# A scan kernel's first product of C and B, moved from behind the transposes into the middle of the next tile's product

## The chip, the cores and the metric

The kernel runs on one core of a Trainium2 chip. The metric is the device time of one execution in microseconds (us). Three executions of the kernel before took 4853.73 to 4854.49 us, with a median of 4853.85 us.

## What is computed

The reference is one layer of a hybrid block: a normalized input goes through one large projection, whose columns feed a state-space scan (SSD) and a second scan (HGRN2); both are mixed, and a large table of experts is applied after that. The change concerns only the SSD scan. Cut to it:

```python
z, xbc, dt_raw, hq, hf, hi, hg, gate_s, gate_h = jnp.split(h @ w_in, split_at, axis=-1)
xbc = jax.nn.silu(causal_dwconv(xbc, conv_w, conv_b))
xs, bm, cm = jnp.split(xbc, [SSD_D_INNER, SSD_D_INNER + SSD_N_GROUPS * SSD_D_STATE], axis=-1)
...
# ssd_chunked, for each of 8 groups of 4 heads, in 4 chunks of 128 tokens
cb = jnp.einsum('bclgn,bcsgn->bgcls', cc, bc)
y_diag = jnp.einsum('bgrcls,bcsgrp->bclgrp', cb[:, :, None] * lmat, xc)
states = jnp.einsum('bcsgn,bgrcs,bcsgrp->bcgrpn', bc, decay_states, xc)
...
y_off = jnp.einsum('bclgn,bcgrpn,bgrcl->bclgrp', cc, states, jnp.exp(a_cum))
```

`cb` is the product of C and B of one chunk (128x128 for one group). It is weighted with the decays of the group's four heads and multiplied with x.

## The kernel before

The SSD stage works through 8 groups in 10 rounds `u`. In round `u`, TensorE makes the six projected tiles of group `u` (`s` = 0 to 5; a tile is 128 features by 512 tokens, 16 steps of 3 matmuls, 48 in all), while the scan of group `p = u - 1` (`comp`) and the end of group `f = u - 2` (`fin`) run between them. Round 0 and round 1 are written out; rounds 2 to 7 are a hardware loop with one body; round 8 has no projection any more, but has six tiles of a gate in its place. So a scan runs in rounds 1 to 8: the first, six in the loop, the last.

**Weights.** A tile of weights comes by a DMA that SP issues into `ring_raw` (two slots). ACT copies it, rounded, to `ring_high` (`split_high`, L258), POOL (GpSimd) subtracts that from the raw tile and writes `ring_low` (`split_low`, L263). TensorE may start a tile once its low half is there (`ring.low_ready`). In ACT's program `split_high` of tile `s + 1` stands at the head of step `s`; in step 1 of a round with `fin` it is followed by the tanh of tile 1 and by `rooted_squares`, a logarithm and an exponential of group `f`. For tile 3 ACT's `split_high` comes right behind those.

**The scan of a group on TensorE.** Behind tile 0 and tile 1 TensorE transposes two tiles of x, behind tile 2 it transposes B (`turn`, L660, into `ps_turn`). VectorE (DVE) copies B out to `b_tok` (L907, counted by `turned_read`). `part_a(p, c)` (L666) is the product of C and B for chunk `c`, and goes into the same `ps_turn`, so it waits for that copy. `part_b(p, c)` (L678 to L684) multiplies the weighted scores with x, and the state; it waits for `mixed_ready`. After tile `s` from 3 on, `part_b(p, s - 3)` and `part_a(p, s - 2)` follow.

**VectorE.** In step 2 it does, in this order: the copy to `b_tok`, the convolution of tile 2 (L808, L810), a sigmoid (L819), `mix(p, 0)` and `make_spans(p, 1)` (L836). Then come step 3's sigmoid and the convolution of tile 3. `mix` waits for ACT's decays and for `part_a`, and is this:

```python
chain.after(v.tensor_tensor(scores[:], ps_turn[:, 0:CH], const["upto"], ALU.mult))
v.tensor_tensor(mixed[:], decay[:], scores[:].unsqueeze(1).to_broadcast([P, HPG, CH]), ALU.mult)
if c < NC - 1:
    v.tensor_tensor(x_dec[:], xdt[:, c].rearrange("p (h d) -> p h d", h=HPG),
                    decay[:, :, CH - 1:CH].to_broadcast([P, HPG, HD]), ALU.mult)
    v.tensor_copy(chunk_dec[:], decay0[:, :, CH - 1])
v.tensor_tensor(c_dec[:], decay0[:],
                act_in[:, 3, c * CH:(c + 1) * CH].unsqueeze(1).to_broadcast([P, HPG, CH]),
                ALU.mult).then_inc(mixed_ready, 1)
```

**ACT.** In steps 2 and later it makes tanh of tile `s`, then the two decays of chunk `s - 2` (L598, L600), and then, at the head of the next step, `split_high` of tile `s + 2`. None of these waits for `part_a(p, 0)`; the decays of chunk 1 wait for `mixed_ready` of chunk 0.

Of the kernel before, what the change touches and what calls it, by code (L numbers as in the profile page):

```python
# [273 lines left out]
def product(nc, out, high, low, x_high, x_low, steps=range(KT), tokens=slice(0, T),  # L274
            wait_piece=None):

    for k in steps:
        if wait_piece is not None and k % PIECE == 0:
            wait_piece(k // PIECE + 1)
        m = slice(k * P, (k + 1) * P)  # L280
        nc.tensor.matmul(out, high[:, m], x_high[:, k, tokens], start=(k == 0), stop=False, skip_group_check=True)  # L281
        nc.tensor.matmul(out, high[:, m], x_low[:, k, tokens], start=False, stop=False, skip_group_check=True)  # L282
        last = nc.tensor.matmul(out, low[:, m], x_high[:, k, tokens], start=False, stop=(k == KT - 1),  # L283
                                skip_group_check=True)
    return last
# [87 lines left out]
def ssd_stage(nc, dram, ring, sent, h, const, streams, norm_mix_w, in_rstd, sums_dram, y_out, gates_out, following):  # L373
# [7 lines left out]
    with ExitStack() as ctx:  # L381
# [54 lines left out]
        turned_read = sem("turned_read")  # L436
# [175 lines left out]
        def _(pe):  # L612
# [7 lines left out]
            def first_tile():  # L620

                pe.wait_ge(ring.low_ready, ring.base + 1)
                pe.wait_ge(acc_read, 1)
                for k in range(KT):
                    pe.wait_ge(x_low, k + 1)
                    tile_done = product(nc, acc[0][:], ring.high[:, 0], ring.low[:, 0], h[0], h[1], range(k, k + 1))
                    if k == DT_FROM:
                        pe.wait_ge(dt_low, 1)
                    for j in range((k - DT_FROM) * KT // (KT - DT_FROM), (k - DT_FROM + 1) * KT // (KT - DT_FROM)):
                        if j >= 0:  # L630
                            dt_done = dt_step(j)
                tile_done.then_inc(ring.used, 1)
                dt_done.then_inc(dt_summed, 1)

            def turn_dt():
                pe.wait_ge(dt_kept, 1)
                for c in range(NC):
                    last = nc.tensor.transpose(ps_turn[:, c * SSD_HEADS:(c + 1) * SSD_HEADS],
                                               y_sq[0:SSD_HEADS, 0, c * CH:(c + 1) * CH],
                                               const["ident"][0:SSD_HEADS, 0:SSD_HEADS])  # L640
                last.then_inc(dt_turned, 1)

            def sum_steps():
                pe.wait_ge(adt_ready, 1)
                for c in range(NC):
                    last = nc.tensor.matmul(ps_turn[0:SSD_HEADS, c * CH:(c + 1) * CH], adt[:, c], const["upto"],
                                            start=True, stop=True)
                last.then_inc(adt_summed, 1)

            def turn_sums():  # L650
                pe.wait_ge(sums_kept, 1)
                for c in range(NC):
                    last = nc.tensor.transpose(ps_turn[:, c * SSD_HEADS:(c + 1) * SSD_HEADS],
                                               sum_rows[:, c * CH:(c + 1) * CH],
                                               const["ident"][0:SSD_HEADS, 0:SSD_HEADS])
                last.then_inc(sums_turned, 1)

            def turn(dst, src, done):
                for c in range(NC):
                    last = nc.tensor.transpose(dst[:, c * P:(c + 1) * P], src[:, c * CH:(c + 1) * CH],  # L660
                                               const["ident"])
                last.then_inc(done, 1)

            def part_a(p, c):
                tok = slice(c * CH, (c + 1) * CH)
                nc.tensor.matmul(ps_turn[:, 0:CH], act_in[:, 2, tok], act_in[:, 3, tok],  # L666
                                 start=True, stop=True).then_inc(a_done, 1)

            def part_b(p, c):
                pe.wait_ge(mixed_ready, NC * p + c + 1)  # L670
                if c == 0:
                    pe.wait_ge(y_read, p + 1)
                else:
                    pe.wait_ge(state_ready, (NC - 1) * p + c)
                for head in range(HPG):
                    part = slice(HD * (head % 2), HD * (head % 2) + HD)
                    o = ps_y[head // 2][part, c * CH:(c + 1) * CH]
                    last = nc.tensor.matmul(o, xdt[:, c, head * HD:(head + 1) * HD], mixed[:, head],  # L678
                                            start=True, stop=(c == 0), skip_group_check=True)
                    if c > 0:  # L680
                        last = nc.tensor.matmul(o, state[:, head], c_dec[:, head], start=False, stop=True,
                                                skip_group_check=True)
                if c < NC - 1:
                    last = nc.tensor.matmul(ps_state[:], b_tok[:, c], x_dec[:].rearrange("p h d -> p (h d)"),  # L684
                                            start=True, stop=True)
                last.then_inc(b_done, 1)

            def body(u, proj, comp, fin, first=False):
                p, f = u - 1, u - 2
                for s in range(SSD_TILES):  # L690
                    n = SSD_TILES * u + s
                    if first and s == 0:
                        first_tile()
                        continue

                    def half(i):
                        return product(nc, acc[s % 2][:], ring.high[:, s % 2], ring.low[:, s % 2], h[0], h[1],
                                       range(i * KT // 2, (i + 1) * KT // 2))

                    def sum_squares():  # L700
                        pe.wait_ge(squared, f + 1)
                        pe.wait_ge(rooted, f + 1)
                        for t in range(2):
                            last = nc.tensor.matmul(ps_squares[:], const["ones"], y_sq[:, t],
                                                    start=(t == 0), stop=(t == 1))
                        last.then_inc(summed, 1)

                    if proj or early(u, s):
                        pe.wait_ge(ring.low_ready, ring.base + n + 1)
                        i = 0 if proj else SSD_TILES * (u - G) + s  # L710
                        if i < 2:
                            pe.wait_ge(acc_read, n + 1)
                        else:
                            pe.wait_ge(gate_read, i - 1)
                        half(0)
                    if s == 0 and fin:
                        part_b(f, NC - 1)
                    if s == 1 and fin and not comp:
                        sum_squares()
                    if first and s == 1:  # L720
                        turn_dt()
                    if first and s == 3:
                        sum_steps()
                    if first and s == 5:
                        turn_sums()
                    if proj or early(u, s):
                        half(1).then_inc(ring.used, 1)
                    if s == 0:
                        if comp:
                            pe.wait_ge(in_ready, p + 1)  # L730
                            turn(ps_turn, act_in[:, 0], turned)
                    if s == 1:
                        if fin and comp:
                            sum_squares()
                        if comp:
                            pe.wait_ge(turned_read, 3 * p + 1)
                            turn(ps_turn, act_in[:, 1], turned)
                    if comp:
                        if s == 2:
                            pe.wait_ge(turned_read, 3 * p + 2)  # L740
                            turn(ps_turn, act_in[:, 2], turned)
                            pe.wait_ge(turned_read, 3 * p + 3)
                            part_a(p, 0)
                        if s > 2:
                            part_b(p, s - 3)
                            part_a(p, s - 2)

            body(0, True, False, False, True)
            body(1, True, True, False)
            with pe.Fori(2, G) as u:  # L750
# [1944 lines left out]
```

## Time and profile before

| | |
|---|---|
| median of 3 runs | 4853.85 us |
| the profiled execution | 4859.09 us |
| its span, first to last instruction | 4857.3 us |
| TensorE (PE) busy | 4780.7 us, 98% of the span |
| VectorE (DVE) busy | 3168.6 us, 65% |
| ACT busy | 1579.4 us, 33% |
| POOL busy | 1316.1 us, 27% |
| mean granted TensorE clock | 0.994 |
| first and last product of C and B (L666) | 146.0 and 720.5 us from the span's start |

The rows give times from the start of the span. "PEld" is TensorE's weight load, which can run beside the matmul ahead of it. A bracket at the end of a row tells how long the engine had been idle before it, and what released it.

### The profile page before, as it was taken

To read this page: it belongs to the slowest core of one execution; us is meant where nothing else is said; L and a number is where in the kernel's file an instruction comes from. 1 tells how busy PE (TensorE), PEld (TensorE's weight loads), DVE (VectorE), ACT (ScalarE), POOL (GpSimd) and SP (SyncE) were. 2 spreads that over 40 slices of the span, in tenths; PEclk is the share of its full clock that TensorE was granted. 3 is DMA by queue.
4 is the path that set the end of the run, shared out by engine and by line. 5 is a ranking of instruction groups with operands and counts; after the bars stand their busy time and mean duration, and the time that the engine had idled before them with its cause. 6 is when DMAs were issued, how large, how long until landed. Compare 5 with 4: busy or idle time off the path is not lost. (4 is left out here: it accounts for less than half of the span.)

```text
span 4857.3 us, 64058 instructions
## 1 busy us (share of the span) xinstructions
PE 4780.7 (98%) x23758; PEld 4133.8 (85%) x23758; DVE 3168.6 (65%) x4246; ACT 1579.4 (33%) x1534; POOL 1316.1 (27%) x549
## 2 busy tenths in 40 slices
PE   8999999999999999999999999999999899999998
PEld 6777788888888787888879999999999788888887
DVE  5676666888878501001168866667674698888888
ACT  3223333333333312212232268822222222222221
POOL 2333330000000043444434442266662111111110
PEclk9999999999999999999999999999999999999999
DMA  3233233222222334334233378799996898888885
GB/s 124 91 108 109 93 122 109 91 82 98 86 94 95 119 125 167 110 127 175 95 129 114 113 246 279 279 339 336 340 340 221 319 337 318 306 297 308 310 297 201
DMA packets 269597, 928.81 MB, mean 191 GB/s; under 512 B 38576, under 2 KB 129200, under 8 KB 191952
## 3 DMA queue, kind: packets, MB, share of 16 engines
q1 hardware_dynamic: 214224, 659.32, 38.9%
q0 software_dynamic: 55296, 268.53, 15.6%
q8 instruction: 41, 0.67, 0.1%
q14 instruction: 36, 0.29, 0.0%
HBM read 849.25 MB, written 78.51 MB: 191 GB/s over the span
## 5 line engine op out<-in xcount | busy, mean ns | idle before, releaser
L263 POOL TENSOR_TENSOR ring_low<-ring_raw,ring_high 128x2048 fp32r<-128x2048 f32 x161 | 754.3, 4685 | 2080.5 <-ACT ring_high L258 2080.5
L281 PE MATMUL rt_acc<-h_high,ring_high 128*128 128x384 f32 (+1 forms) x2304 | 790.8, 343 | 5.9 <-POOL ring_low L263 3.2
L282 PE MATMUL rt_acc<-h_low,ring_high 128*128 128x384 f32 (+1 forms) x2304 | 785.1, 341 | 0.0
L283 PE MATMUL rt_acc<-h_high,ring_low 128*128 128x384 f32 (+1 forms) x2304 | 784.9, 341 | 0.0
L258 ACT ACTIVATE ring_high<-ring_raw 128x2048 fp32r<-128x2048 f32 x337 | 644.9, 1914 | 392.1 <-PE mix_s_acc L283 126.8
L281 PEld LDWEIGHTS rt_acc<-h_high,ring_high 128*128 128x128 f32 x2304 | 433.3, 188 | 18.8 <-DVE h_low L301 5.0
L283 PEld LDWEIGHTS rt_acc<-h_high,ring_low 128*128 128x128 f32 x2304 | 433.2, 188 | 10.4
L282 PEld LDWEIGHTS rt_acc<-h_low,ring_high 128*128 128x128 f32 x2304 | 433.4, 188 | 9.4
L281 PE MATMUL hg_acc<-h_high,ring_high 128*128 128x512 f32 x1088 | 433.6, 399 | 2.1 <-DVEq L1253 1.6
L283 PE MATMUL hg_acc<-h_high,ring_low 128*128 128x512 f32 x1088 | 425.6, 391 | 0.0
L282 PE MATMUL hg_acc<-h_low,ring_high 128*128 128x512 f32 x1088 | 423.9, 390 | 0.0
L2238 DVE TENSOR_TENSOR ring_low<-ring_raw,ring_high 128x2048 fp32r<-128x2048 f32 x107 | 245.3, 2293 | 263.4 <-ACT ring_high L258 263.4
L1743 POOL DMA_INDIRECT sb_op_rows<-v_tiles,row_of x128 | 120.7, 943 | 977.1 <-DVE x_tok_back L2429 849.8
L281 PE MATMUL ssd_acc<-h_high,ring_high 128*128 128x512 f32 x896 | 357.0, 398 | 9.1 <-DVE h_low L301 5.7
L282 PE MATMUL ssd_acc<-h_low,ring_high 128*128 128x512 f32 x896 | 350.5, 391 | 0.0
L283 PE MATMUL ssd_acc<-h_high,ring_low 128*128 128x512 f32 x896 | 350.5, 391 | 0.0
L2429 DVE SCALAR_TENSOR_TENSOR x_tok_back<-sb_op_rows,own_weight,x_tok_back 128x2048 f32<-128x2048 f32 x128 | 300.4, 2347 | 0.0
L1743 POOL DMA_INDIRECT x_mid_front<-u_rows,row_of x128 | 199.3, 1557 | 353.0 <-DVE sb_rt_dot L2219 332.5
L2219 DVE CUSTOM_DVE_ANT_0 x_mid_front<-x_mid_front,sb_rt_h_tok 128x2048 f32<-128x2048 f32 x128 | 292.7, 2287 | 0.0
L2453 DVE TENSOR_TENSOR x_tok_back<-x_tok_back,op_out 128x512 f32<-128x512 f32 x384 | 261.5, 683 | 43.4 <-PE op_out L2411 40.7
L1947 POOL DMA_INDIRECT gates_added<-sb_rt_added_gate,sb_rt_added_at x128 | 241.5, 1887 | 52.8 <-issue 37.8
L1976 ACT ACTIVATE sent_gelu<-rt_acc 128x384 f32<-128x384 f32 x128 | 63.0, 493 | 560.4 <-PE rt_acc L283 560.3
(330 smaller groups left out, 9683.8 us busy)
## 6 DMA issues: line engine op xcount, KB each, us to landing
ring_raw<-u_tiles SPq DMA_DIRECT2D x128, 1024.0 KB, 5.1
ring_raw<-v_tiles SPq DMA_DIRECT2D x128, 1024.0 KB, 6.2
ring_raw<-w_hg SPq DMA_DIRECT2D x64, 1024.0 KB, 4.9
ring_raw<-w_ssd SPq DMA_DIRECT2D x48, 1024.0 KB, 6.6
ring_raw<-w_mix_s SPq DMA_DIRECT2D x32, 1024.0 KB, 5.4
ring_raw<-w_mix_h SPq DMA_DIRECT2D x32, 1024.0 KB, 4.9
gelu<-sent_gelu SPq DMA_DIRECT2D x128, 192.0 KB, 4.9
weights_gelu<-gelu SPq DMA_DIRECT2D x32, 768.0 KB, 8.2
```

The source lines that it names most:

```text
L258: nc.scalar.activation(ring.high[:, slot], ring.raw[:, slot], ACT.Copy).then_inc(ring.high_ready, 1)
L263: nc.gpsimd.tensor_tensor(ring.low[:, slot], ring.raw[:, slot], ring.high[:, slot].bitcast(F32), ALU.subtract).then_inc(ring.low_ready, 1)
L281: nc.tensor.matmul(out, high[:, m], x_high[:, k, tokens], start=(k == 0), stop=False, skip_group_check=True)
L282: nc.tensor.matmul(out, high[:, m], x_low[:, k, tokens], start=False, stop=False, skip_group_check=True)
L283: last = nc.tensor.matmul(out, low[:, m], x_high[:, k, tokens], start=False, stop=(k == KT - 1), skip_group_check=True)
L1743: return pool.indirect_dma_start(rows[0:OWN, slot], None, table, bass.IndirectOffsetOnAxis(ap=row_of[0:OWN, k:k + 1], axis=0))
L1947: pool.indirect_dma_start(scratch["gates_added"].rearrange("i j (t a) -> (i j t) a", a=1), bass.IndirectOffsetOnAxis(ap=added_at[:, e:e + ...
L1976: nc.scalar.activation(gelu[:, s], acc[s][:, 0:REST], ACT.Gelu).then_inc(acc_read, 1)
L2219: vec.tensor_tensor_reduce(rows[0:OWN, slot], rows[0:OWN, slot], h_tok[0:OWN], 1.0, 0.0, ALU.mult, ALU.add, dot[0:OWN, slot:slot + 1]).the ...
L2238: vec.tensor_tensor(ring.low[:, slot], ring.raw[:, slot], ring.high[:, slot].bitcast(F32), ALU.subtract).then_inc(ring.low_ready, 1)
L2429: vec.scalar_tensor_tensor(x_tok[0:OWN, 0], rows[0:OWN, slot], weight[0:OWN, ds(k, 1)], x_tok[0:OWN, 0], ALU.mult, ALU.add).then_inc(summe ...
L2453: vec.tensor_tensor(x, x, ps_out[(2 * OUTS * buf + OUTS * half + i) % BANKS][:], ALU.add).then_inc(out_added, 1)
```

## The change

TensorE's product of C and B for the first chunk of a group, `part_a(p, 0)`, with its wait for the copy of B, is taken from behind the transposes of B at the end of step 2 and put between the two halves (24 matmuls each) of tile 3's product. Nothing is added or removed, and no other engine's program is changed; no DMA is moved.

```diff
@@ -715,6 +715,9 @@
                         half(0)
                     if s == 0 and fin:
                         part_b(f, NC - 1)
+                    if s == 3 and comp:
+                        pe.wait_ge(turned_read, 3 * p + 3)
+                        part_a(p, 0)
                     if s == 1 and fin and not comp:
                         sum_squares()
                     if first and s == 1:
@@ -739,8 +742,6 @@
                         if s == 2:
                             pe.wait_ge(turned_read, 3 * p + 2)
                             turn(ps_turn, act_in[:, 2], turned)
-                            pe.wait_ge(turned_read, 3 * p + 3)
-                            part_a(p, 0)
                         if s > 2:
                             part_b(p, s - 3)
                             part_a(p, s - 2)
```

TensorE's instructions in the loop's body, at the end of tile 2 and the start of tile 3, before the change (a REGISTER_ALU row works out the value that the next wait compares with):

```order
L283 MATMUL ssd_acc<-h_high,ring_low 128x512
L740 REGISTER_ALU
L660 MATMUL ssd_ps_turn<-c_ident,streams 128x128 x4
L742 REGISTER_ALU
L666 MATMUL ssd_ps_turn<-streams 128x128
L709 REGISTER_ALU
L281 MATMUL ssd_acc<-h_high,ring_high 128x512
```

The same place in the changed kernel:

```order
L283 MATMUL ssd_acc<-h_high,ring_low 128x512
L743 REGISTER_ALU
L660 MATMUL ssd_ps_turn<-c_ident,streams 128x128 x4
L709 REGISTER_ALU
L281 MATMUL ssd_acc<-h_high,ring_high 128x512
L282 MATMUL ssd_acc<-h_low,ring_high 128x512
```

The product L666 is gone from between the transposes and tile 3; the next wait of TensorE behind the transposes is now that of tile 3 itself. The middle of tile 3 in the changed kernel, with the 24th matmul of the tile in the second row:

```order
L282 MATMUL ssd_acc<-h_low,ring_high 128x512
L283 MATMUL ssd_acc<-h_high,ring_low 128x512
L719 REGISTER_ALU
L666 MATMUL ssd_ps_turn<-streams 128x128
L281 MATMUL ssd_acc<-h_high,ring_high 128x512
L282 MATMUL ssd_acc<-h_low,ring_high 128x512
```

There the product has arrived, 24 matmuls later in TensorE's order than before. At the end of tile 3 the order is as it was.

## Rows read from the trace of the kernel before

**Rows 1.** Waits of the weight loader, 120 to 740 us: us in total, times, longest

```profile
PEld ssd_ps_turn L666 <- DVE sb_ssd_b_tok L907: 8.2, 8, 1.0
...
PEld ssd_acc L281 <- POOL ring_low L263: 1.4, 6, 0.2
```

**Rows 2.** Timeline of PE, a loop round, from the transposes of B to tile 3

```profile
451.05 0.60 PE L660 MATMUL ssd_ps_turn<-c_ident,streams 128*128 128x128 f32 x4
452.43 0.49 PE L666 MATMUL ssd_ps_turn<-streams 128*128 128x128 f32 x2 [0.78 <-DVE sb_ssd_b_tok L907]
452.97 0.50 PE L281 MATMUL ssd_acc<-h_high,ring_high 128*128 128x512 f32 x1
453.31 0.40 PE L282 MATMUL ssd_acc<-h_low,ring_high 128*128 128x512 f32 x1
```

**Rows 3.** Timeline of PE, transposes of x behind tile 0, the same round

```profile
426.62 0.60 PE L660 MATMUL ssd_ps_turn<-c_ident,streams 128*128 128x128 f32 x4
...
427.29 0.40 PE L282 MATMUL ssd_acc<-h_low,ring_high 128*128 128x512 f32 x1
```

**Rows 4.** Timeline of POOL, the same round: low halves of tiles 3 and 4

```profile
448.35 4.57 POOL L263 TENSOR_TENSOR ring_low<-ring_raw,ring_high 128x2048 fp32r<-128x2048 f32 x1 [9.48 <-ACT ring_high L258]
459.36 4.65 POOL L263 TENSOR_TENSOR ring_low<-ring_raw,ring_high 128x2048 fp32r<-128x2048 f32 x1 [6.45 <-ACT ring_high L258]
```

**Rows 5.** Timeline of DVE, the same round: mix of chunk 0 and the spans

```profile
457.51 0.29 DVE L855 TENSOR_TENSOR sb_ssd_scores<-ssd_ps_turn,c_upto 128x128 f32<-128x128 f32 x1 [1.41 <-ACT sb_ssd_decay L600]
457.84 0.69 DVE L856 TENSOR_TENSOR sb_ssd_mixed<-sb_ssd_decay,sb_ssd_scores 128x512 f32<-128x512 f32 x1
...
458.85 0.69 DVE L861 TENSOR_TENSOR sb_ssd_c_dec<-sb_ssd_decay,streams 128x512 f32<-128x512 f32 x1
459.45 5.23 DVE L836 TENSOR_SCALAR sb_ssd_span_log<-sb_ssd_sums,sb_ssd_sum_at 128x128 f32<-128x128 f32 x4
```

**Rows 6.** Timeline of PE, the same round: middle of tile 3, then its end

```profile
458.58 0.39 PE L281 MATMUL ssd_acc<-h_high,ring_high 128*128 128x512 f32 x1
...
464.11 0.66 PE L678 MATMUL ssd_ps_y<-sb_ssd_mixed,sb_ssd_xdt 128*64 128x128 f32 x8
...
465.24 0.38 PE L666 MATMUL ssd_ps_turn<-streams 128*128 128x128 f32 x2
465.38 0.48 PE L281 MATMUL ssd_acc<-h_high,ring_high 128*128 128x512 f32 x1
465.69 0.39 PE L282 MATMUL ssd_acc<-h_low,ring_high 128*128 128x512 f32 x1
```

**Rows 7.** Timelines of DVE and POOL in round 1, from 113 us

```profile
115.31 5.52 DVE L883 TENSOR_TENSOR streams<-streams 128x1024 f32<-128x1024 f32 x1
...
113.70 6.04 POOL L263 TENSOR_TENSOR ring_low<-ring_raw,ring_high 128x2048 fp32r<-128x2048 f32 x1 [6.93 <-ACT ring_high L258]
```

**Rows 8.** Timelines of PE, DVE and POOL in round 1, first scan

```profile
144.63 0.60 PE L660 MATMUL ssd_ps_turn<-c_ident,streams 128*128 128x128 f32 x4
...
146.58 0.39 PE L282 MATMUL ssd_acc<-h_low,ring_high 128*128 128x512 f32 x1
...
150.77 0.29 DVE L855 TENSOR_TENSOR sb_ssd_scores<-ssd_ps_turn,c_upto 128x128 f32<-128x128 f32 x1 [1.40 <-ACT sb_ssd_decay L600]
...
152.62 4.63 POOL L263 TENSOR_TENSOR ring_low<-ring_raw,ring_high 128x2048 fp32r<-128x2048 f32 x1 [8.82 <-ACT ring_high L258]
```

**Rows 9.** Timelines of PE, DVE and POOL in round 8, last scan

```profile
682.67 0.47 PE L281 MATMUL ssd_acc<-h_high,ring_high 128*128 128x512 f32 x1
682.99 0.39 PE L282 MATMUL ssd_acc<-h_low,ring_high 128*128 128x512 f32 x1
...
683.02 0.29 DVE L855 TENSOR_TENSOR sb_ssd_scores<-ssd_ps_turn,c_upto 128x128 f32<-128x128 f32 x1 [0.65 <-PE ssd_ps_turn L666]
...
684.76 4.75 POOL L263 TENSOR_TENSOR ring_low<-ring_raw,ring_high 128x2048 fp32r<-128x2048 f32 x1 [5.54 <-ACT ring_high L258]
```

**Rows 10.** Window with all eight scans: busy us of each engine, PEclk, DMA

```profile
118.00:736.00 618.00, 611.45 (x3020) 491.89 (x3020) 403.12 (x557) 189.44 (x199) 228.96 (x50) 1.00 0.31 105
```

## The prediction

> **What bounds the kernel now.** I read the window over all eight scans first: TensorE is busy 611.45 of 618 us at a granted clock of 1.00 [rows 10], so a microsecond that TensorE is held there is a microsecond of the time. Then the waits of its weight loader [rows 1]: the product that the change moves stands idle eight times, 1.0 us each, for the copy of B. That is what the change goes after. The reader should see the row below it too: six times tile 3's first weights wait 0.2 us for POOL's low half. Small as it is, it says that in the six loop rounds tile 3 could not have started earlier, whatever stood in front of it. The timelines show it. POOL's subtraction for tile 3 runs from 448.35 to 452.92, and tile 3 starts at 452.97 [rows 4, 2]. In the first and the last scan there is no such wait.
>
> **What the change gives, by round.** Where nothing holds TensorE, it is 0.67 us from the start of four transposes to the second matmul of the next tile [rows 3]; behind the transposes of B it is 2.26 us [rows 2]. So 1.59 us stand there for the moved product and its wait.
> In the first scan this distance is 146.58 - 144.63 = 1.95 [rows 8]: without the product it should be 0.67, a gain of 1.28. The last scan's rows have the same form [rows 9]; I take 1.28 there too.
> In the six loop rounds I take a gain of nothing. TensorE comes to tile 3 at about 451.5 and waits for POOL until 452.97, as before. POOL's time is set by ACT, whose rounding copy for tile 3 stands behind the logarithm and the exponential of `rooted_squares`; all of that hangs on the end of tile 1, which the change does not touch.
>
> **What the product costs in its new place.** From L666 to the second matmul behind it is 465.69 - 465.24 = 0.45, when nothing is waited for [rows 6]. With one step of 0.23 from the matmul in front, that is 0.68 where two plain steps take 0.46, so 0.23 us. The bounds are 0.2 (its own streaming) and 0.65 (0.88 from L666 to the second matmul after a stop, in [rows 2]). I take 0.23: the copy of B is long done there, so no stop is due. First and last scan together: 2 x (1.28 - 0.23) = 2.1 us gained.
>
> **Who is late next.** `mix(p, 0)` on DVE waits for the product and for ACT's decays. Before, the product is early and the decays decide, at 457.51 [rows 5]. Now the product comes behind the 24th matmul, where a matmul starts at 458.58 [rows 6]. In the last scan the scores start 0.35 after the matmul that follows the product [rows 9], and that matmul follows it by 0.14 [rows 6]. So in a loop round the scores start at 458.58 + 0.14 + 0.35 = 459.07, which is 1.56 later.
> By itself this is harmless: `c_dec` would end at 459.54 + 1.56 = 461.1, and `part_b` asks for it only at 464.11 [rows 6], or 464.34 with the 0.23 above. But POOL starts its subtraction for tile 4 at 459.36 and ends at 464.01 [rows 4]; that time doesn't move, as nothing that ACT does before it waits for the product. Before, `mix` was just through: `c_dec` started at 458.85, and the spans behind it were caught, four small instructions in 5.23 us [rows 5]. Now `mixed`, the second instruction of `mix`, comes to 459.07 + 0.33 = 459.40, and finds POOL at work.
> Does a TENSOR_TENSOR wait for POOL as the spans do? One row says yes: L883, both inputs in SBUF, started at 115.31 with POOL's subtraction running from 113.70 to 119.74, and took 5.52 us [rows 7]. At `c_dec`'s pace (0.69 for 512 elements) its 1024 need 1.3, so it ran only from about POOL's end on. `mixed`, `x_dec` and `c_dec` have both inputs in SBUF as well.
> The Trainium skill, page "SBUF — State Buffer", section "Who interferes with whom", says that a DVE instruction with two SBUF inputs contends with a GpSimd instruction that reads SBUF, and that whichever is first keeps the other out to its end. By that rule `mixed` waits here, and the change loses in the loop; the trace agrees, with the 5.52 us of L883.
>
> So in a loop round `mixed` runs from about 463.9. From its start to the end of `c_dec` it is 459.54 - 457.84 = 1.70 [rows 5], so `mixed_ready` comes at 465.6, and `part_b` starts 1.5 us later than at 464.11. The 0.23 lie inside this. It doesn't matter much who wins at 459.36 against 459.40: if `mixed` slips in first, POOL starts up to 0.65 later, ends near 464.65, and `x_dec` to `c_dec` (1.09) end at 465.7.
> The bounds of this term: 0.23 (nobody blocks), 0.6 (only the COPY and the spans are blocked: `chunk_dec` waits, and `c_dec` ends at 464.7), and 2.3 (below).
> What is late behind it has cover: the convolution of tile 3 and with it ACT's decays, its split for tile 5 and POOL come some 1.9 us later, TensorE 1.5; and the next tile 3 is tied to its own tile 1.
>
> **First scan.** Tile 3's second matmul moves to 145.30, its 25th to 145.30 + (458.58 - 453.31) = 150.57, the scores to 151.06 instead of 150.77 [rows 8]. `c_dec` starts 1.34 after the scores, at 152.40, and POOL at 152.62: it just gets through. It then holds POOL up to 0.5, so tile 4's low half comes at about 157.7, and TensorE is there at 157.6. I take 0.1 off: 0.9 gained. If the 0.2 us of room are not there, `c_dec` ends near 157.9, where `part_b` stood at 146.58 + 10.80 = 157.4, and the scan loses 0.5 instead.
> **Last scan.** The scores come at about 687.5, inside POOL's subtraction (684.76 to 689.51 [rows 9]), so `mix` ends at 689.4 + 1.7 = 691.1. `part_b` asks at 681.7 + 10.8 + 0.2 = 692.7. No wait: 1.0 gained.
>
> **The sum.** 6 x 1.5 - 0.9 - 1.0 = 7.1 us more. The profiled execution took 4859.09, so 4866.2 by it; it stands 5.24 above the median of the runs, so 4861.0 for the median, 0.15% above 4853.85. No other stage is touched; they follow TensorE and shift with it.
>
> **The rivals.**
> - *Plain gain*, 0.04: TensorE's 1.0 us comes free in all eight, because POOL's row against tile 3 is a coincidence. 8 x 1.05 = 8.4 less: 4845.5. Against it: [rows 1] name POOL six times, exactly the loop rounds.
> - *Tile 3 is tied to POOL, but nobody blocks `mix`*, 0.04: 6 x 0.23 - 2.1 = -0.7: 4853.1. The 5.52 of L883 speaks against it.
> - *Only the COPY is blocked*, 0.08: 6 x 0.6 - 1.9 = 1.7: 4855.6. L883 speaks against it, but it is one row.
> - *A longer block*, slower, 0.09. Place: POOL's subtraction for tile 4. With a DVE instruction in front, POOL's took 6.04 us in [rows 7] instead of 4.65. If `mixed` slips in first and POOL takes that, it ends at 465.4, and `x_dec` to `c_dec` at 466.4: 2.3 a round, 6 x 2.3 - 1.9 = 11.9: 4865.8. It decides from 1.93 a round on, (9.7 + 1.9) / 6.
> - *The clock falls*, slower, 0.05: TensorE now stands twice in 13 us, about 1.5 before tile 3 and 1.3 behind it. If the granted clock fell to half for half a tile (5.5 us) each round, that would be 33 us: 4894. Before, eight waits of 1.0 us leave it at 1.00 [rows 10].
> - *My forecast*, 0.70, with a range of its own of 4858.5 to 4863.5 (1.1 to 1.9 a round; the first scan gains or loses).
>
> **How the numbers follow.** A measurement of this kernel can tell about 0.2%, 9.7 us, from no change. The range 4855 to 4866 takes in my forecast, the COPY rival and the longer block: 0.87, less some 0.05 at its edges. Faster by over 0.2% needs the plain gain and 1.2 us or more in each scan: 0.02. Slower by over 0.2% is the longer block, the clock, and a little of my own case: 0.16. Within 0.2%: 0.82.
>
> **What the changed profile would show.** In the loop rounds: tile 3's first matmul still directly behind POOL's end, now with about 1.4 us of waiting for POOL; the scores released by L666 and no longer by ACT; `mixed` (L856) with about 5.2 us instead of 0.69 in six rounds and in the last; `part_b` waiting about 1.3 us for `c_dec`; the period of a round 1.5 longer. In the first scan no long `mixed`. The prediction is wrong if `mixed` keeps 0.69 in the loop, if tile 3 starts earlier than POOL's end allows (then POOL was ahead), or if tile 5 or the next round picks up a new wait.

## The result, and the profile after

In 20 executions of each, the changed kernel takes a median of 4861.53 us (4857.83 to 4869.19) and the kernel before 4856.09 us (4851.88 to 4858.94). The medians are 5.4 us apart. The ratio is 1.0013 with a 95% interval of 1.0007 to 1.0019: slower by 0.13%, which is less than the 0.2% by which I called a change measurable, but the interval leaves out no change at all. The forecast was 4861.0 and 0.15%. That 4861.0 is so near to 4861.53 is in part luck: the forecast stood on 4853.85 for the kernel before, and its 20 executions came out 2.2 us above that. The difference was forecast as 7.1 us and measured as 5.4.

Single executions of one kernel spread by 7 to 11 us, so a profiled span can't be read for this change: that of after (4856.5 us) is even shorter than that of before. The stage itself repeats far better. I take as **the stage** the time from the first scan's first transposes (L660) to the last product of C and B (L666), both read on TensorE's timeline. Before it is 720.54 - 121.91 = 598.63 us, after it is 725.65 - 120.35 = 605.30 us: 6.67 more, where the forecast's sum was 7.1. Each stage is read from one trace, but its rounds repeat: from the transposes of B in one loop round to those in the next it is 76.62 to 76.70 us before.

The waits of TensorE and its weight loader in the changed kernel, 120 to 745 us (us in total, times, longest), with the shorter waits left out; they answer to [rows 1]:

```profile
PEld ssd_acc L281 <- POOL ring_low L263: 9.3, 6, 1.6
PEld ssd_ps_y L678 <- DVE sb_ssd_c_dec L862: 9.2, 6, 1.5
PE ssd_acc L281 <- POOL ring_low L263: 7.9, 6, 1.3
PE ssd_ps_y L678 <- DVE sb_ssd_c_dec L862: 6.7, 6, 1.1
```

The eight waits for the copy of B are gone. In six rounds POOL has taken their place in front of tile 3, and behind tile 3 six new waits for VectorE's `c_dec` have appeared. Below is one loop round on TensorE; the rows answer to [rows 2] and [rows 6], and lines of the changed file from 718 on have a higher number than before:

```profile
452.81 0.60 PE L660 MATMUL ssd_ps_turn<-c_ident,streams 128*128 128x128 f32 x4
454.73 0.50 PE L281 MATMUL ssd_acc<-h_high,ring_high 128*128 128x512 f32 x1 [1.32 <-POOL ring_low L263]
...
460.35 0.38 PE L666 MATMUL ssd_ps_turn<-streams 128*128 128x128 f32 x2
467.34 0.66 PE L678 MATMUL ssd_ps_y<-sb_ssd_mixed,sb_ssd_xdt 128*64 128x128 f32 x8 [1.12 <-DVE sb_ssd_c_dec L862]
```

The same round on VectorE, and POOL's subtraction for tile 4; they answer to [rows 5] and [rows 4]:

```profile
460.83 0.29 DVE L856 TENSOR_TENSOR sb_ssd_scores<-ssd_ps_turn,c_upto 128x128 f32<-128x128 f32 x1 [2.97 <-PE ssd_ps_turn L666]
461.16 5.12 DVE L857 TENSOR_TENSOR sb_ssd_mixed<-sb_ssd_decay,sb_ssd_scores 128x512 f32<-128x512 f32 x1
466.20 0.41 DVE L859 TENSOR_TENSOR sb_ssd_x_dec<-sb_ssd_xdt,sb_ssd_decay 128x256 f32<-128x256 f32 x1
466.54 0.16 DVE L861 COPY sb_ssd_chunk_dec<-sb_ssd_decay 128x4 f32<-128x4 f32 x1
466.61 0.68 DVE L862 TENSOR_TENSOR sb_ssd_c_dec<-sb_ssd_decay,streams 128x512 f32<-128x512 f32 x1
...
461.12 4.60 POOL L263 TENSOR_TENSOR ring_low<-ring_raw,ring_high 128x2048 fp32r<-128x2048 f32 x1 [6.45 <-ACT ring_high L258]
```

The scores are now released by the product and no longer by ACT, 8.02 us behind the start of the transposes of B (before 6.46). `mixed` meets POOL's subtraction 0.04 us after its start, and takes 5.12 us instead of 0.69.

That is the picture in two of the six loop rounds. In the other four `mixed` is the first of the two, by at most 0.03 us, and `x_dec` is caught in its place:

```profile
304.90 0.69 DVE L857 TENSOR_TENSOR sb_ssd_mixed<-sb_ssd_decay,sb_ssd_scores 128x512 f32<-128x512 f32 x1
305.51 4.83 DVE L859 TENSOR_TENSOR sb_ssd_x_dec<-sb_ssd_xdt,sb_ssd_decay 128x256 f32<-128x256 f32 x1
...
304.93 5.13 POOL L263 TENSOR_TENSOR ring_low<-ring_raw,ring_high 128x2048 fp32r<-128x2048 f32 x1 [6.46 <-ACT ring_high L258]
...
311.08 0.66 PE L678 MATMUL ssd_ps_y<-sb_ssd_mixed,sb_ssd_xdt 128*64 128x128 f32 x8 [1.11 <-DVE sb_ssd_c_dec L862]
```

POOL's instruction is then recorded with 5.13 us instead of 4.60, so it has waited for `mixed` in turn, and TensorE's wait is the same to 0.01.

### The profile page after: what moved, and what is told of

Its sections match the earlier page's. It is cut to its first block and busy times, and to the rows that moved or that the text cites. A ratio compares the mean times of both kernels' runs of the same rounds, so it can differ in the third digit from the quotient of the medians.

```text
span 4856.5 us, 64058 instructions
## 1 busy us (share of the span) xinstructions
PE 4771.5 (98%) x23758; PEld 4127.4 (85%) x23758; DVE 3169.8 (65%) x4246; ACT 1579.5 (33%) x1534; POOL 1315.8 (27%) x549
```

## The experiments

Each experiment is one more edit to one of the two kernels, timed beside the kernel before on the same chip. The table has the stage of each as its one trace shows it; what was expected stands with each below. Four kernels have intervals that take in 1: for them the times alone tell nothing, and the reading rests on the stage. In all eleven the difference of the stage and that of the medians agree within 1.3 us.

| kernel | stage, us | to before | ratio of times, 95% interval |
|---|---|---|---|
| before | 598.63 | | |
| the change | 605.30 | +6.67 | 1.0013 (1.0007 to 1.0019) |
| before, early rounding copy | 596.58 | -2.05 | 0.9996 (0.9987 to 1.0005) |
| change, early rounding copy | 588.86 | -9.77 | 0.9981 (0.9972 to 0.9990) |
| change in the outer two rounds alone | 596.52 | -2.11 | 0.9996 (0.9987 to 1.0005) |
| change in the six loop rounds alone | 607.36 | +8.73 | 1.0018 (1.0009 to 1.0027) |
| product behind the 12th matmul | 598.27 | -0.36 | 0.9999 (0.9990 to 1.0008) |
| product behind the 36th matmul | 609.48 | +10.85 | 1.0020 (1.0011 to 1.0029) |
| change, scores in PSUM | 601.92 | +3.29 | 1.0008 (0.9999 to 1.0017) |
| 12th matmul, early rounding copy | 588.66 | -9.97 | 0.9979 (0.9970 to 0.9988) |
| change, POOL held back | 614.97 | +16.34 | 1.0037 (1.0023 to 1.0050) |
| 36th matmul, early rounding copy | 616.99 | +18.36 | 1.0035 (1.0021 to 1.0049) |

### Which rounds gain and which lose

Two kernels have the product moved in some rounds only. `type(u) is int` holds for the written-out rounds, and the second kernel has the opposite:

```diff
-                    if s == 3 and comp:
+                    if s == 3 and comp and type(u) is int:
                         pe.wait_ge(turned_read, 3 * p + 3)
                         part_a(p, 0)
...
                             turn(ps_turn, act_in[:, 2], turned)
+                            if not (type(u) is int):
+                                pe.wait_ge(turned_read, 3 * p + 3)
+                                part_a(p, 0)
```

> The product is moved only in the two written-out rounds (first and last scan); the six loop rounds keep it behind the transposes. My theory: -1.0 in each of the two, nothing else: stage 596.6, time -2 us. Rival (the gain of the outer rounds is not there, the whole +6.67 of the stage is a smaller loss in all eight): 600.3.

> The product is moved only in the six loop rounds. My theory: +1.43 in each of six: stage 607.2, time +8.6 us (+0.18%). Rival (a smaller loss in all eight): 603.6.

Measured: 596.52 and 607.36. The loop rounds lose 1.45 each, and the two effects add up to the change: -2.11 + 8.73 = 6.62, against 6.67. A loss spread over all eight is out. What each outer round gains is read best from its own stretch. From the transposes of B in the first scan to those in the next round it is 76.35 us before and 75.36 with the product moved, so 0.99. From the last transposes of B to the last product of C and B it is 39.49 and 38.52, so 0.97. The other 0.15 of the 2.11 lies in the six rounds that this edit leaves alone; so small a difference in a stage means nothing.

### Is tile 3 held by POOL?

ACT's rounding copy of tile 3 is put ahead of tile 1's tanh and of the logarithm and exponential, in the loop rounds; first in the kernel before:

```diff
-                    if (proj or early(u, s)) and not (first and s == 0):
+                    ahead = proj and fin
+                    if (proj or early(u, s)) and not (first and s == 0) and not (ahead and s == 2):
                         split_high(nc, act, ring, (s + 1) % 2, SSD_TILES * u + s + 1, 3 * u + (s + 1) // 2)
+                    if ahead and s == 1:
+                        split_high(nc, act, ring, 1, SSD_TILES * u + 3, 3 * u + 1)
```

> The kernel before, with one change on ACT alone: in the six loop rounds the rounding copy of tile 3 (split_high) stands ahead of tile 1's tanh and of the logarithm and exponential, not behind them. I measure the stage in the trace from the first scan's first transposes (L660) to the last product of C and B (L666): 598.63 us before, 605.30 with the change. My theory (tile 3 is held by POOL's low half): tile 3 starts directly behind the product of C and B as in the first scan, 0.31 us earlier in each of six rounds: stage 596.7, time -1.9 us (-0.04%, not to be told in the times). Rival (tile 3 was not held by POOL): 598.6.

Measured: 596.58. The six waits for POOL are gone from the trace, and the stage is shorter by 2.05, 0.34 a round. So the 0.2 us of [rows 1] were a real hold on TensorE, and not a coincidence. How firm a bound POOL is shows when the product goes as well. The same edit in the changed kernel:

> The changed kernel with ACT's early rounding copy of tile 3 in the loop rounds. My theory: POOL is done some 8 us earlier, tile 3 starts behind the transposes, 1.59 us earlier than before, the product costs 0.23, the scores come at about the time at which ACT's decays are done, and mix is through before POOL's next subtraction: -1.36 in each of six rounds and -2.1 in the outer two: stage 588.4, time about -10 us (-0.2%). Room for c_dec ahead of POOL is some 0.5 us. Rival A (the block of mix has nothing to do with where tile 3 starts, it comes with the product's new place): mixed still takes 5.1 us in the loop and part_b waits: stage 598 to 600. Rival B (the early copy makes a new wait, on VectorE's sigmoid behind POOL's earlier subtraction, that reaches TensorE): over 590 with a wait of the transposes.

Measured: 588.86. TensorE waits in the stage neither for POOL nor for `c_dec`. VectorE and POOL in a loop round of this kernel:

```profile
451.10 0.29 DVE L859 TENSOR_TENSOR sb_ssd_scores<-ssd_ps_turn,c_upto 128x128 f32<-128x128 f32 x1 [1.41 <-ACT sb_ssd_decay L603]
451.43 0.69 DVE L860 TENSOR_TENSOR sb_ssd_mixed<-sb_ssd_decay,sb_ssd_scores 128x512 f32<-128x512 f32 x1
...
452.44 0.69 DVE L865 TENSOR_TENSOR sb_ssd_c_dec<-sb_ssd_decay,streams 128x512 f32<-128x512 f32 x1
...
452.95 4.62 POOL L263 TENSOR_TENSOR ring_low<-ring_raw,ring_high 128x2048 fp32r<-128x2048 f32 x1 [14.58 <-ACT ring_high L258]
```

The scores wait for ACT's decays again, `mixed` takes 0.69, and `c_dec` starts 0.5 us before POOL. The stage is 9.77 below that of the kernel before. Of these 2.05 are the early copy's own, and 7.72 are the moved product's: with tile 3 free to start, the same move that cost 6.67 gains 7.72. It is 0.96 in each loop round (76.34 to 75.38 us) and 0.98 and 0.97 in the outer ones. Rivals A and B are both out.

### Does the loss depend on where in tile 3 the product stands?

The product stands behind 12 or 36 of the tile's 48 matmuls instead of 24. The kernel for 12 (the changed kernel's product between the halves is taken out; the other likewise in the second half):

```diff
                     def half(i):
-                        return product(nc, acc[s % 2][:], ring.high[:, s % 2], ring.low[:, s % 2], h[0], h[1],
-                                       range(i * KT // 2, (i + 1) * KT // 2))
+                        steps = range(i * KT // 2, (i + 1) * KT // 2)
+                        if s == 3 and comp and i == 0:
+                            product(nc, acc[s % 2][:], ring.high[:, s % 2], ring.low[:, s % 2], h[0], h[1], range(0, 4))
+                            pe.wait_ge(turned_read, 3 * p + 3)
+                            part_a(p, 0)
+                            steps = range(4, KT // 2)
+                        return product(nc, acc[s % 2][:], ring.high[:, s % 2], ring.low[:, s % 2], h[0], h[1], steps)
...
-                    if s == 3 and comp:
-                        pe.wait_ge(turned_read, 3 * p + 3)
-                        part_a(p, 0)
```

> The product stands behind the 12th matmul of tile 3 instead of the 24th, in all eight scans. My theory (the loss is a race between mix and POOL's subtraction for tile 4): the product comes 2.7 us earlier, mix waits for ACT's decays again and is through before POOL; mixed keeps 0.69 in the loop, part_b waits for nothing. Left are +0.23 in six rounds, as tile 3 still waits for POOL, and -1.05 in the outer two: stage 597.9, time -0.7 us. Rival (splitting tile 3's product with a foreign product is what costs): stage 605 as with the change.

Measured: 598.27. Tile 3 still waits for POOL in six rounds (9.3 us in the weight loader's waits, as with the change), but no wait for `c_dec` is left. VectorE and POOL in a loop round:

```profile
455.95 0.69 DVE L859 TENSOR_TENSOR sb_ssd_mixed<-sb_ssd_decay,sb_ssd_scores 128x512 f32<-128x512 f32 x1
...
456.97 0.69 DVE L864 TENSOR_TENSOR sb_ssd_c_dec<-sb_ssd_decay,streams 128x512 f32<-128x512 f32 x1
...
457.48 4.65 POOL L263 TENSOR_TENSOR ring_low<-ring_raw,ring_high 128x2048 fp32r<-128x2048 f32 x1 [6.46 <-ACT ring_high L258]
```

A loop round takes 76.94 us on average, against 76.68 before. So a product inside a tile costs about 0.27, where I had taken 0.23. Interrupting the tile is not what costs.

> The product stands behind the 36th matmul of tile 3, in all eight scans. My theory: in the loop mixed comes 2.7 us later, still inside POOL's subtraction, and is released at the same moment: mixed takes 2.4 us instead of 5.1, and the loss stays +1.43 a round. The first scan now falls into the block too: part_b waits about 2.4 us there, +1.4 instead of -1.0. Stage 607.7, time +9 us. Rival (the loss grows with the delay of the product): 2.7 more in each of six rounds, stage over 620.

Measured: 609.48. `mixed` takes 2.38 to 2.45 us in the six loop rounds, and TensorE's wait for `c_dec` stays at 1.11 to 1.18: the block ends when POOL does, however late VectorE runs into it. One of these rounds:

```profile
469.44 2.38 DVE L859 TENSOR_TENSOR sb_ssd_mixed<-sb_ssd_decay,sb_ssd_scores 128x512 f32<-128x512 f32 x1
...
466.69 4.59 POOL L263 TENSOR_TENSOR ring_low<-ring_raw,ring_high 128x2048 fp32r<-128x2048 f32 x1 [6.45 <-ACT ring_high L258]
```

`mixed` ends at 471.82, which is 0.54 behind POOL's end. The rival, a loss that grows with the delay, is out. The first scan is caught as expected, with a wait of 2.40. But the stage is 1.8 longer than expected, and nearly all of that is no wait. TensorE's timeline behind that wait:

```profile
158.75 0.66 PE L678 MATMUL ssd_ps_y<-sb_ssd_mixed,sb_ssd_xdt 128*64 128x128 f32 x8 [2.40 <-DVE sb_ssd_c_dec L864]
...
160.78 0.63 PE L283 MATMUL ssd_acc<-h_high,ring_low 128*128 128x512 f32 x1
161.21 0.63 PE L281 MATMUL ssd_acc<-h_high,ring_high 128*128 128x512 f32 x1
...
163.74 0.39 PE L281 MATMUL ssd_acc<-h_high,ring_high 128*128 128x512 f32 x1
163.97 0.39 PE L282 MATMUL ssd_acc<-h_low,ring_high 128*128 128x512 f32 x1
```

The matmuls come every 0.43 us instead of 0.23 until 163.7. From 158 to 166 us the windows show a granted clock of 0.79 on average; it is 1.00 on both sides. This is the clock rival of the prediction, in a place where it was not forecast. The price is 1.6 us: from these transposes of B to the next it is 79.40 us, and 77.81 in the last but one experiment below, where the same scan has the same wait (2.39) and the clock stays at 1.00.

### What in `mix` waits for POOL?

In the changed kernel the masked scores are written to PSUM, behind the state's columns (`ps_state` is made 128 columns wider for that, and its other uses name their own columns; these lines are left out):

```diff
-                chain.after(v.tensor_tensor(scores[:], ps_turn[:, 0:CH], const["upto"], ALU.mult))
-                v.tensor_tensor(mixed[:], decay[:], scores[:].unsqueeze(1).to_broadcast([P, HPG, CH]), ALU.mult)
+                chain.after(v.tensor_tensor(ps_state[:, HPG * HD:HPG * HD + CH], ps_turn[:, 0:CH], const["upto"], ALU.mult))
+                v.tensor_tensor(mixed[:], decay[:], ps_state[:, HPG * HD:HPG * HD + CH].unsqueeze(1).to_broadcast([P, HPG, CH]), ALU.mult)
```

> The changed kernel with the masked scores written to PSUM instead of SBUF, so that mixed has one input in SBUF and one in PSUM; x_dec and c_dec keep two in SBUF. If two SBUF inputs are what makes a DVE instruction wait for POOL: mixed runs through POOL's subtraction in 0.7 us, x_dec waits instead (about 4.5 us), mixed_ready comes 0.6 earlier: +0.8 a round, stage 601.6. Rival (every TENSOR_TENSOR waits while POOL works): mixed takes 5.1 us, stage 605.3. Rival (only reads by broadcast or copies wait): x_dec takes 0.42, stage under 600.

Measured: 601.92. VectorE, POOL and TensorE in a loop round of this kernel:

```profile
461.12 0.69 DVE L857 TENSOR_TENSOR sb_ssd_mixed<-sb_ssd_decay,ssd_ps_state 128x512 f32<-128x512 f32 x1
461.73 4.29 DVE L859 TENSOR_TENSOR sb_ssd_x_dec<-sb_ssd_xdt,sb_ssd_decay 128x256 f32<-128x256 f32 x1
465.94 0.16 DVE L861 COPY sb_ssd_chunk_dec<-sb_ssd_decay 128x4 f32<-128x4 f32 x1
...
461.13 4.61 POOL L263 TENSOR_TENSOR ring_low<-ring_raw,ring_high 128x2048 fp32r<-128x2048 f32 x1 [6.46 <-ACT ring_high L258]
...
466.75 0.66 PE L678 MATMUL ssd_ps_y<-sb_ssd_mixed,sb_ssd_xdt 128*64 128x128 f32 x8 [0.57 <-DVE sb_ssd_c_dec L862]
```

Here `mixed` starts 0.01 before POOL, so its own 0.69 would not prove much; but POOL tells it. POOL's instruction takes 4.61, not the 5.13 that it takes when a `mixed` with both inputs in SBUF has started in front of it. In the other five loop rounds `mixed` starts 0.01 behind POOL, and takes 0.69 all the same:

```profile
306.04 0.69 DVE L857 TENSOR_TENSOR sb_ssd_mixed<-sb_ssd_decay,ssd_ps_state 128x512 f32<-128x512 f32 x1
...
306.03 4.62 POOL L263 TENSOR_TENSOR ring_low<-ring_raw,ring_high 128x2048 fp32r<-128x2048 f32 x1 [6.44 <-ACT ring_high L258]
```

With both inputs in SBUF a start as close behind POOL is enough to be caught: in the kernel with the change in the loop rounds alone, a `mixed` that started at 305.86, with POOL at 305.85, took 5.13. And `x_dec`, with both inputs in SBUF, waits in all six rounds of this kernel (4.28 or 4.29). The Trainium skill, page "SBUF — State Buffer", section "Who interferes with whom", says that a DVE instruction with two SBUF inputs contends with a GpSimd instruction that reads SBUF, and one with at most one SBUF input (outside the modes that use both ports) does not. The trace agrees with both halves: `x_dec` waits, and `mixed` with its scores in PSUM does not.

### Can POOL be kept out of the way instead?

In the changed kernel ACT's rounding copy of tile 4 waits for `mix(p, 0)` in the loop rounds, so that POOL starts later:

```diff
+                    if s == 3 and proj and fin:
+                        act.wait_ge(mixed_ready, NC * p + 1)
                     if (proj or early(u, s)) and not (first and s == 0):
                         split_high(nc, act, ring, (s + 1) % 2, SSD_TILES * u + s + 1, 3 * u + (s + 1) // 2)
```

> The changed kernel with one wait more on ACT in the six loop rounds: its rounding copy of tile 4 waits for mix(p, 0), so that POOL's subtraction can't meet it. My theory: mixed takes 0.69 again and part_b waits for nothing, but POOL's subtraction for tile 4 now ends at about mix's end + 1.9 + 4.7 us, which is some 2.2 us after tile 4 could start: the wait moves from part_b to tile 4's first weights and grows, +2.4 a round: stage 611. If a wait of over 2 us lets the granted clock fall, as in the first scan of the run with the product behind the 36th matmul (a 2.4 us wait, then a pitch of 0.43 us for some 3.4 us), it is up to 1.6 more a round: 611 to 621. Rival (POOL's time is not what hurts): stage under 605.

Measured: 614.97. `mixed` takes 0.69 again, and the wait has moved to tile 4's first weights:

```profile
457.90 0.50 PE L281 MATMUL ssd_acc<-h_high,ring_high 128*128 128x512 f32 x1 [1.31 <-POOL ring_low L263]
...
472.76 0.50 PE L281 MATMUL ssd_acc<-h_high,ring_high 128*128 128x512 f32 x1 [1.97 <-POOL ring_low L263]
```

A round that has both costs 2.5 us against before. After two of the six waits of 1.97 the clock fell as well: the window from 474 to 480 us shows 0.74, and those from 630 to 636 and from 636 to 642 show 0.84 and 0.87. These two rounds take 80.78 us and the other four 79.17 to 79.23.

### The block alone, without a late tile 3

The kernel with the product behind the 36th matmul gets the early rounding copy too; both edits are shown above.

> The product behind the 36th matmul of tile 3, and ACT's early rounding copy of tile 3 in the loop. Tile 3 starts without a wait, so this shows the block alone. My theory: mix is caught by POOL in each loop round, mixed_ready comes at POOL's end + 1.7, and part_b stands ready 1.36 earlier than before, so it waits about 2.9 us: +1.5 a round, and with the clock falling behind a wait of that length (1.6 us in the first scan of the run without the early copy) +3.1 a round. Stage 598.6 + 6 x 3.1 + 3.05 - 1.0 = 619; without the fall of the clock 609 to 611. Rival (the early copy heals the change wherever the product stands): 588.

Measured: 616.99. TensorE waits 2.7 us for `c_dec` in each loop round. So the early copy heals the change only as long as `mix` gets through before POOL; the rival is out. I had expected a fall of the clock of 1.6 us in each loop round and in the first scan. It fell in four of the six loop rounds and not in the first scan, and a fall can cost more than 1.6, so that 616.99 lies near the expected 619 partly by luck. The waits of four neighbouring loop rounds:

```profile
237.21 0.66 PE L681 MATMUL ssd_ps_y<-sb_ssd_mixed,sb_ssd_xdt 128*64 128x128 f32 x8 [2.70 <-DVE sb_ssd_c_dec L867]
...
315.34 1.12 PE L681 MATMUL ssd_ps_y<-sb_ssd_mixed,sb_ssd_xdt 128*64 128x128 f32 x8 [2.71 <-DVE sb_ssd_c_dec L867]
...
396.47 0.83 PE L681 MATMUL ssd_ps_y<-sb_ssd_mixed,sb_ssd_xdt 128*64 128x128 f32 x8 [2.71 <-DVE sb_ssd_c_dec L867]
...
476.19 0.66 PE L681 MATMUL ssd_ps_y<-sb_ssd_mixed,sb_ssd_xdt 128*64 128x128 f32 x8 [2.71 <-DVE sb_ssd_c_dec L867]
```

From the first of these waits to the second it is 78.13 us, with a clock of 1.00. From the second, whose eight small matmuls already take 1.12 instead of 0.66, to the third it is 81.13, and from the third to the fourth 79.72.

### The better version

Product behind the 12th matmul, with the early rounding copy; the edits are those above.

> The product behind the 12th matmul of tile 3 and ACT's early rounding copy of tile 3 in the loop rounds. My theory: as the changed kernel with the early copy, but without the near tie between the scores and the decays: -1.36 in six rounds, -1.05 in the outer two: stage 588.4, time -10 us (-0.21%). Rival: tile 4 is now held by POOL's next low half, which ends at the moment at which tile 4 would start; then the stage is 589 to 590.

Measured: 588.66, and 4845.30 us against 4854.98. It is as fast as the changed kernel with the early copy (588.86), and tile 4 has no wait for POOL, so the rival is out. What is larger is the room between the product and the scores that read it: in a loop round the product starts 3.3 us before the scores (447.60 and 450.86), and with the product behind the 24th matmul 0.5 us (450.56 and 451.10). The scores wait for ACT's decays in both kernels, and `c_dec` starts 0.5 us ahead of POOL in both. Both beat the kernel before by about 0.2%.

## Why the prediction was right

The forecast was right in sign and size, and its steps hold one by one.

- **No gain in the loop, since tile 3 waits for POOL.** Right. I expected about 1.4 us of waiting where the product had been; it is 1.32 on the matmul and 1.6 on the weight loader. The changed kernel with the early rounding copy shows it from the other side: without that wait each loop round gains.
- **The product's price in the middle of a tile, 0.23.** Slightly low: 0.27 from the kernel with the product behind the 12th matmul. In the change it is hidden inside the longer wait.
- **`mix` is next, 1.56 later in the loop.** Right: the scores stand 8.02 behind the transposes' start, 459.07 - 451.05 = 8.02 by the prediction.
- **It meets POOL, and it hardly matters who is first.** Right, and the tie of 0.04 us was a true one: two rounds went one way, four the other. The "longer block" rival had the order of the four, but not its length: POOL took 5.13, not 6.04.
- **1.5 a round.** 1.43 by the timelines of after: from the transposes of B in one round to those in the next it is 452.81 - 374.71 = 78.10, and it was 451.05 - 374.38 = 76.67.
- **0.9 and 1.0 in the outer rounds.** 0.99 and 0.97. The first scan got through before POOL, as taken (`c_dec` at 150.84, POOL at 151.07); the 0.1 for tile 4 did not come. In the last scan `mixed` is caught (2.13 us) and nobody waits for it.
- **The sum, 7.1.** 6.67, mostly since a loop round loses 1.44 on average and not 1.5. The agreement of the time itself, 4861.0 and 4861.53, is closer than the steps are, and in part luck.
- **The clock rival.** It didn't happen in the changed kernel, whose windows in the stage all show 1.00. It did in three of the experiments, where a fall cost 1.6 to 3.0 us; the rival's 5.5 a round was too high a price.

That the block comes from the use of two SBUF inputs is shown for `mixed`, which stopped waiting when one input was moved to PSUM. For `x_dec` and `c_dec` it is argued from the same rule, as I didn't move their inputs.

## What to carry to other kernels

A wait of 0.2 us in the table can hide a bound that takes away the whole gain of a change, as it did here in six rounds of eight: before taking work away in front of an instruction, look at how close the next thing that it waits for ended. When an instruction is moved to fill a hole, its reader moves too; ask what else the reader's engine will meet at the new time, here POOL's subtraction, where coming 1.56 us later made one instruction of VectorE 4.4 us longer and held TensorE for 1.1. And when a move fails because a second chain is late, repair that chain (here one instruction of ACT, moved ahead) before giving the move up: the same move of the product, which cost 6.7 us of the stage, then gained 7.7 on top of the repair's own 2.1.

## What the runs showed of the hardware

- A VectorE instruction and a POOL instruction that both read SBUF on two inputs, started at most 0.04 us apart, go one after the other, in either order: `mixed` took 5.12 when POOL (4.60) was first, and POOL took 5.13 when `mixed` (0.69) was. Where POOL was first, `mixed` ended 0.54 to 0.56 us behind POOL's end, however late it had run into it, in all traces here (466.28 and 465.72 in the changed kernel, 471.82 and 471.28 behind the 36th matmul). In these traces the wait lies inside the instruction's own duration, so a table of waits doesn't show it.
- Whether TensorE's granted clock falls from 2.4 to 1.2 GHz (0.50 in the window from 474 to 476 us of the kernel with POOL held back) behind a wait is not settled by the length of the wait alone. After waits of 1.1 to 1.3 us it never fell in these traces; after 1.97 it fell in two of six loop rounds, after 2.7 in four of six, after 2.4 in one of two. What decides between them is open. A fall cost 1.6 to 3.0 us. That is why such a kernel's loss does not grow evenly with its waits.
